# One feed-forward pass over both segments in the first layer, and the two halves of the recurrence's inverse extended separately

## What is computed

```python
h_lat = h_lat + m_lat[5] * channel_mixer(_modulate(_rms_norm(h_lat, norm_ffn[i]), m_lat[3], m_lat[4]))
if update_ctx:
    h_ctx = h_ctx + m_ctx[5] * channel_mixer(_modulate(_rms_norm(h_ctx, norm_ffn[i]), m_ctx[3], m_ctx[4]))

def _swiglu(h, w1, w3, w2):
    return (jax.nn.silu(h @ w1) * (h @ w3)) @ w2
```

## Time and profile before

| | us |
|---|---|
| median of three runs | 3259.41 |
| lowest and highest of them | 3255.51, 3261.84 |
| the profiled execution's own time | 3247.96 |
| its span, first to last instruction | 3246.2 |
| TensorE busy, share of the span | 3035.9, 94% |
| VectorE busy | 2022.0, 62% |
| ScalarE busy | 1500.8, 46% |
| mean granted TensorE clock | 0.967 |

### The profile page before, as it was taken

One profiled execution on the slowest core, in us unless ns is written; L12 is line 12 of the kernel. 1 busy time (PEld: TensorE's weight loads), 2 busy tenths in 40 slices (PEclk: granted clock), 3 DMA queues, 4 the chain that ended last, 5 costly groups with the idle time before them and its releaser, 6 DMA issues.

```text
span 3246.2 us, 70881 instructions
## 1 busy us (share of the span) xinstructions
PE 3035.9 (94%) x28960; PEld 2343.0 (72%) x28960; DVE 2022.0 (62%) x3676; ACT 1500.8 (46%) x2394; POOL 7.7 (0%) x17
## 2 busy tenths in 40 slices
PE   5988897989999989989999999999999999999998
PEld 3866684878989977643333333359988999998998
DVE  3768757565555552766666666666685666667566
ACT  3334223223444442646666666664447444445543
POOL 0000000000000000000000000000000000000000
PEclk8998898999999999989999999999999999999999
DMA  5232205004545552059999999955542555543454
GB/s 212 97 130 111 106 3 227 4 25 139 181 155 175 182 180 91 21 224 379 379 378 389 377 380 407 373 229 184 181 143 99 181 182 172 182 155 122 145 181 155
DMA packets 132792, 619.71 MB, mean 191 GB/s; under 512 B 14496, under 2 KB 18080, under 8 KB 98400
## 3 DMA queue, kind: packets, MB, share of 16 engines
q1 hardware_dynamic: 132048, 610.18, 51.5%
q0 software_dynamic: 528, 6.43, 0.5%
HBM read 615.50 MB, written 1.05 MB: 190 GB/s over the span
## 4 chain that ended last, share of the span: by engine, by line
PE 82%; DVE 10%; ACT 3%; DMA 2%; issue 1%; SPq 1%; DVEq 0%; ACTq 0%
PE ps L2443 21%; PE ps L310 16%; PE ps L311 16%; PE ps L312 16%; DMA ada_late<-wada 1%; PE ps L1777 1%; PE ps L864 1%; DVE w_lo L273 1%; PE ps L1774 1%; PE ps L1768 1%; PE ps L2454 1%; DVE tt L1865 1%; ACT w_hi L269 1%; DVE mxv L2157 1%; PE ps L792 0%
## 5 line engine op out<-in xcount | busy, mean ns | idle before, releaser
L273 DVE TENSOR_TENSOR w_lo<-w_raw,w_hi 128x1024 fp32r<-128x1024 f32 x529 | 646.3, 1224 | 598.3 <-ACT w_hi L269 594.7
L310 PE MATMUL ps<-a_hi,w_hi 128*128 128x256 f32 (+1 forms) x3012 | 899.1, 299 | 48.4 <-DVE a_lo L811 11.9
L311 PE MATMUL ps<-a_lo,w_hi 128*128 128x256 f32 (+1 forms) x3012 | 895.2, 297 | 0.0
L312 PE MATMUL ps<-a_hi,w_lo 128*128 128x256 f32 (+1 forms) x3012 | 894.4, 297 | 0.0
L269 ACT ACTIVATE w_hi<-w_raw 128x1024 fp32r<-128x1024 f32 x529 | 557.7, 1056 | 610.4 <-PE ps L312 556.3
L310 PEld LDWEIGHTS ps<-a_hi,w_hi 128*128 128x128 f32 x3012 | 578.2, 192 | 71.9 <-issue 45.4
L312 PEld LDWEIGHTS ps<-a_hi,w_lo 128*128 128x128 f32 x3012 | 573.0, 190 | 16.1
L311 PEld LDWEIGHTS ps<-a_lo,w_hi 128*128 128x128 f32 x3012 | 573.2, 190 | 15.2 <-issue 0.5
L2625 DVE COPY wx<-wset 128x512 f32 x1188 | 425.1, 422 | 223.1 <-PE ps L2443 208.0
L2565 ACT ACTIVATE wx<-wset 128x512 f32 x792 | 444.4, 621 | 214.7 <-PE ps L2443 206.3
L2443 PE MATMUL ps<-wx,xT 128*32 128x512 f32 x2640 | 377.6, 596 | 4.8 <-DVE wx L2625 4.8
(11 more groups left out here) (518 smaller groups left out, 3444.1 us busy)
## 6 DMA issues: line engine op xcount, KB each, us to landing
w_raw<-wstream SPq DMA_DIRECT2D x529, 512.0 KB, 3.3
wset<-wexp SPq DMA_DIRECT2D x264, 1024.0 KB, 7.8
ada_late<-wada SPq DMA_DIRECT2D x80, 512.0 KB, 6.2
ada_raw<-wada SPq DMA_DIRECT2D x16, 512.0 KB, 9.2
bia<-bias POOLq DMA_DIRECT2D x1, 4096.0 KB, 13.4
con<-consts SPq DMA_DIRECT2D x1, 1824.0 KB, 16.0
conb<-constsb POOLq DMA_DIRECT2D x1, 1224.0 KB, 5.7
hT<-ctxT SPq DMA_DIRECT2D x1, 1024.0 KB, 12.3
```

Source lines behind the costliest of these rows:

```text
L273: nc.vector.tensor_tensor(wlo[:, slot, :], raw[:, slot, :], whi[:, slot, :].bitcast(F32), ALU.subtract).then_inc(lo_ready.sem, 1)
L310: nc.tensor.matmul(out, lhs[0], rhs[0], start=start, stop=False, skip_group_check=skip)
L311: nc.tensor.matmul(out, lhs[0], rhs[1], start=False, stop=False, skip_group_check=skip)
L312: return nc.tensor.matmul(out, lhs[1], rhs[0], start=False, stop=stop, skip_group_check=skip)
```

## The change

Both segments go through the first layer's feed-forward in one pass. The stream has one entry `ffn` of 66 tiles in place of two. One norm of 512 columns precedes it (the routines that the attention's norm uses). All 44 tiles of `w1` and `w3` go first, alternately, each with 24 matmuls of 512 columns into bank 5, 6 or 7 in rotation; the 22 hidden blocks of both segments are all kept, in new tiles `gs_hi` and `gs_lo`. Then come 22 tiles of `w2` in a new order, with output group m as the outer index: one bank per group, filled completely over 22 hidden blocks before the next group begins. Group m's sum is added to `hT` as soon as it is complete. The engines' lists for this pass are written out without loops.

In the recurrence, half 1 of each level goes to bank 6+d in place of the second half of bank 2+d. VectorE adds the halves with two instructions of 256 columns. The add of half 0 raises `lv_in` itself. The add of half 1 raises a new signal `t1_in`, on which TensorE waits before it uses `tt` as an operand of L1774 and L1777 in the next level.

```diff
-STREAM = [("w_in", 27), ("w_out", 8), ("ffn_ctx", 3 * FT), ("ffn_lat", 3 * FT), ("qkv", 24),
+STREAM = [("w_in", 27), ("w_out", 8), ("ffn", 3 * FT), ("qkv", 24),
...
+        def pe_ffn_both(pe, base):
+            a = a_cols([CTX, LAT])
+            def chunk(t, k, out, operand, first, last):
+                slot = (base + t) % RING
+                w = (whi[:, slot, k * P:(k + 1) * P], wlo[:, slot, k * P:(k + 1) * P])
+                return pe_triple(out, w, operand, first, last)
+            def h_chunk(t, k):
+                last = chunk(t, k, ps[:, 5 + (base + t) % RING, :], a(k), k == 0, k == KT - 1)
+                if k == KT - 1:
+                    last.then_inc(tile_used.sem, 1)
...
+            for t in range(RING, 2 * FT):
+                pe.wait_ge(lo_ready.sem, base + t + 1)
+                f, third = divmod(t - RING, 2)
+                pe.wait_ge((S("g_f") if third else S("silu_ready")).sem, f + 1)
+                for k in range(KT):
+                    h_chunk(t, k)
+            for t in range(2 * FT, 3 * FT):
+                pe.wait_ge(lo_ready.sem, base + t + 1)
+                for j in range(KT):
+                    m, f = divmod((t - 2 * FT) * KT + j, FT)
+                    if m == 0 and j == 0:
+                        pe.wait_ge(S("g_ready").sem, min(f + KT, FT))
+                    last = chunk(t, j, ps[:, m, :], (gs_hi[:, f, :], gs_lo[:, f, :]), f == 0, f == FT - 1)
+                    if j == KT - 1:
+                        last.then_inc(tile_used.sem, 1)
+                    elif f == FT - 1:
+                        last.then_inc(*S("pair_out").one)
...
+        def dve_ffn_both(dve, link, base):
+            for t in range(3 * FT):
+                if t >= 1:
+                    dve_split(dve, base + t + LEAD, (base + t + LEAD) % RING)
+                if t < 2 * FT and t % 2 == 1:
+                    f = t // 2
+                    dve.wait_ge(S("silu_ready").sem, f + 1)
+                    dve.wait_ge(tile_used.sem, used(base, t))
+                    nc.vector.tensor_tensor(gf2[:, f % 2, :], sil2[:, f % 2, :], ps[:, 5 + (base + t) % RING, :],
+                                            ALU.mult).then_inc(S("g_f").sem, 1)
...
+                for m in range(KT):
+                    if 2 * FT + (m * FT + FT - 1) // KT == t:
...
+                        for s in (CTX, LAT):
+                            dst = hT[:, m, seg_cols(s)]
+                            ins = nc.vector.scalar_tensor_tensor(dst, ps[:, m, seg_cols(s)], m_col(0, 5, m, s), dst,
+                                                                 ALU.mult, ALU.add)
...
@@ pe_solve
                 for d in range(2):
                     pe.wait_ge(*S("x_sb").next("pe"))
+                    if lv > 0:
+                        pe.wait_ge(*S("t1_in").next("pe"))
                     if lv < RLEV - 1:
                         heads_of(d, lambda d, m, e: nc.tensor.matmul(
                             ps[hp(e), 2 + d, col(m)], tt[hp(e), d, 1, m, :], xs[hp(e), d, m, :],
-                            start=True, stop=True))
+                            start=True, stop=True)).then_inc(*S("t_ps").one)
                     heads_of(d, lambda d, m, e: nc.tensor.matmul(
-                        ps[hp(e), 2 + d, col(m, 1)], xs[hp(e), d, m, :], tt[hp(e), d, 1, m, :],
-                        start=True, stop=True)).then_inc(*S("t_ps").one)
+                        ps[hp(e), 6 + d, col(m)], xs[hp(e), d, m, :], tt[hp(e), d, 1, m, :],
+                        start=True, stop=True)).then_inc(*S("t1_ps").one)
@@ dve_solve
                 for d in range(2):
-                    dve.wait_ge(*S("t_ps").next("dve"))
                     if lv < RLEV - 1:
-                        t2_ = tt[:, d, :, :, :].rearrange("p s m l -> p (s m) l")
-                        link(nc.vector.tensor_tensor(t2_, t2_, bank(2 + d, 0, 8), ALU.add))
-                        dve.sem_inc(S("lv_in").sem, 1)
-                    else:
-                        nc.vector.tensor_tensor(tt[:, d, 1, :, :], tt[:, d, 1, :, :], bank(2 + d, 1), ALU.add
-                                                ).then_inc(*S("tT_done").one)
+                        dve.wait_ge(*S("t_ps").next("dve"))
+                        nc.vector.tensor_tensor(tt[:, d, 0, :, :], tt[:, d, 0, :, :], bank(2 + d), ALU.add
+                                                ).then_inc(*S("lv_in").one)
+                    dve.wait_ge(*S("t1_ps").next("dve"))
+                    nc.vector.tensor_tensor(tt[:, d, 1, :, :], tt[:, d, 1, :, :], bank(6 + d), ALU.add
+                                            ).then_inc(*S("t1_in" if lv < RLEV - 1 else "tT_done").one)
@@ the order of the stages, TensorE
-            for s, nm in ((CTX, "ffn_ctx"), (LAT, "ffn_lat")):
-                pe_norm(pe)
-                pe_ffn(pe, BASE[nm], s, FT)
+            pe_norm2(pe)
+            pe_ffn_both(pe, BASE["ffn"])
             pe_norm2(pe)
             pe_qkv(pe)
```

More of the change, by code:

```diff
@@ L110 @@
           "x_out": ("st_ps", 6), "slot_ps": ("g_ps", 8), "slot_sb": ("mb_rt", 1), "moe_free": ("mb_r", 1), "x_scaled": ("e1", 16),
+          "t1_ps": ("bc_ps", 16), "t1_in": ("wm", 16),
           "r_ready": ("e2", 16), "r_ps": ("dd", 16)}
@@ L365, in a_cols @@
             return lambda k: (a_hi[:, k, c], a_lo[:, k, c])
[L369 to L420, removed]
@@ L617, in dve_ffn_late @@
             split(3 * F - 1, 3 * F - 1)
+        def pe_ffn_both(pe, base):
[8 more added lines that the diff above has]
+                    last.then_inc(tile_used.sem, 1)
+            for j in range(RING):
+                pe.wait_ge(lo_ready.sem, base + j + 1)
+            for j, k in head_order(range(RING)):
+                if j == 0:
+                    pe.wait_ge(*S("alo_ready").next("pe"))
+                h_chunk(j, k)
+            for t in range(RING, 2 * FT):
[15 more added lines that the diff above has]
+                        last.then_inc(*S("pair_out").one)
+            gcount["pe"] += FT
@@ new lines, in act_ffn_both @@
+        def act_ffn_both(act, base):
+            for t in range(3 * FT):
+                if t >= 1:
+                    n = base + t + LEAD
+                    act_split(act, n, n // RING, n % RING)
+                if t < 2 * FT and t % 2 == 0:
+                    f = t // 2
+                    act.wait_ge(tile_used.sem, used(base, t))
+                    if f >= 2:
+                        act.wait_ge(S("g_f").sem, f - 1)
+                    nc.scalar.activation(sil2[:, f % 2, :], ps[:, 5 + (base + t) % RING, :], ACT.Silu
+                                         ).then_inc(S("silu_ready").sem, 1)
+            gcount["act"] += FT
@@ new lines, in dve_ffn_both @@
+        def dve_ffn_both(dve, link, base):
+            for t in range(3 * FT):
+                if t >= 1:
+                    dve_split(dve, base + t + LEAD, (base + t + LEAD) % RING)
+                if t < 2 * FT and t % 2 == 1:
+                    f = t // 2
+                    dve.wait_ge(S("silu_ready").sem, f + 1)
+                    dve.wait_ge(tile_used.sem, used(base, t))
+                    nc.vector.tensor_tensor(gf2[:, f % 2, :], sil2[:, f % 2, :], ps[:, 5 + (base + t) % RING, :],
+                                            ALU.mult).then_inc(S("g_f").sem, 1)
+                    dve.wait_ge(S("g_f").sem, f + 1)
+                    nc.vector.tensor_copy(gs_hi[:, f, :], gf2[:, f % 2, :]).then_inc(S("g_hi").sem, 1)
+                    dve.wait_ge(S("g_hi").sem, f + 1)
+                    nc.vector.tensor_tensor(gs_lo[:, f, :], gf2[:, f % 2, :], gs_hi[:, f, :].bitcast(F32),
+                                            ALU.subtract).then_inc(S("g_ready").sem, 1)
+                for m in range(KT):
+                    if 2 * FT + (m * FT + FT - 1) // KT == t:
+                        if (m * FT + FT - 1) % KT == KT - 1:
+                            dve.wait_ge(tile_used.sem, used(base, t))
+                        else:
+                            dve.wait_ge(*S("pair_out").next("dve"))
+                        for s in (CTX, LAT):
+                            dst = hT[:, m, seg_cols(s)]
+                            ins = nc.vector.scalar_tensor_tensor(dst, ps[:, m, seg_cols(s)], m_col(0, 5, m, s), dst,
+                                                                 ALU.mult, ALU.add)
+                            if s == CTX:
+                                link(ins)
+                        ins.then_inc(*S("h_ready").one)
+            gcount["dve"] += FT
@@ L619, in build @@
         gcount = {"pe": 0, "act": 0, "dve": 0}
         xcount = {"act": 0}
[L622 to L689, removed]
@@ L826, in build @@
         normw2 = sb("normw2", [P, KT, T2], at=arena)
+        gs_hi = sb("gs_hi", [P, FT, T2], F32R, at=arena + 4 * KT * T2)
+        gs_lo = sb("gs_lo", [P, FT, T2], F32R, at=arena + 4 * KT * T2 + 4 * FT * T2)
+        sil2 = sb("sil2", [P, 2, T2], at=g_at)
+        gf2 = sb("gf2", [P, 2, T2], at=g_at + 8 * T2)
```

(20 more changed lines are left out.)

## The result

The changed kernel takes 3222.9 us (median of four runs, 3222.0 to 3224.1) against 3260.6 of the kernel before in the same comparison (3255.5 to 3263.5). The ratio is 0.9886, 95% interval 0.9871 to 0.9902, so the gain is 37.7 us with an interval of 32 to 42. The forecast was 3229, and the measured time lies inside the range of 3218 to 3243. In a later comparison on one chip the same kernel stood at 3219.8 against 3257.1, ratio 0.9890 (0.9875 to 0.9905).

The account below looks back on a forecast made before the run. TensorE, busy 94% of the span, was taken as the bound. Feed-forward 19.2 us plus recurrence 11.2 us made 30.4 us, taken from the median 3259.4 to give 3229 us, range 3218 to 3243.

Parts of the forecast that it names:

- What bounds the kernel: Whole kernel: TensorE, busy 94% of the span, is the bound; halving weight splits and loads is worth nothing by itself.
- The pace: Feed-forward: 3168 narrow matmuls at 0.1200 us become 1584 wide ones at 0.2333 us, a gain of 10.6 us.
- The edges: Feed-forward: one norm of 13.97 us replaces 7.77 and 12.61; with its norm the pass takes 386.1 instead of 405.3 us.
- The recurrence: Levels of the recurrence: period falls from 3.40 to 3.05 us, over 32 transitions, a gain of 11.2 us.
- The reason inside the level: Recurrence level: half 0's add of 256 columns, 0.42 us, right after its group lets TensorE's products start at 0 and 0.467.
- the spare of 0.08 us for direction 1: Recurrence level: VectorE signals direction 1's first add at about 3.44 us, needed at 3.52.
- The sum and the median: Whole kernel: 19.2 + 11.2 = 30.4 us saved, taken from the median 3259.4 rather than the profiled 3247.96, giving 3229 us.
- VectorE late: Rival, recurrence levels: VectorE's in-order list misses the spare; full loss of that gain gives 3240 us; chance 0.14.
- Wide no faster: Rival, feed-forward pass: wide matmuls no faster than narrow, with operands from two large new tiles; 3240 us; chance 0.06.
- The rule's pace: Rival, feed-forward pass: 512 columns run at the skill page's 0.216 us; 3201 us; chance 0.02.
- Starvation: Rival, feed-forward pass: TensorE's list without loops waits for instructions; at 0.7 us a tile, 3275 us; chance 0.04.
- No effect: Rival, the passes: some dependence, such as tiles sharing memory, serialises them to no gain; 3255 to 3260 us; chance 0.02.

Follow-up runs that it names:

- narrow matmuls: Changed kernel, but each wide feed-forward product done as two of 256 columns with the same weight; 3232.3 us, ratio 0.9937 to the kernel before.
- short norms: Changed kernel with its two norms beside the feed-forward summed in four strips, root and reciprocal on 128 columns; 3211.4 us, ratio 0.9862 to the kernel before.
- late add: Changed kernel, but VectorE adds half 0 only when both halves of its direction are there; 3227.1 us, ratio 0.9921 to the kernel before.
- written-out loops: Kernel before with the loops of its two feed-forward passes written out on TensorE, ScalarE and VectorE, nothing else; 3257.1 us, ratio 1.0009.

## Why the prediction was right, and where it was off

**What bounds the kernel.** Right. Halving the weight splits and the loads shows in busy time and DMA share and in no wait of TensorE, and it leaves the pass at 382.2 us while the matmuls stay narrow.

**The pace.** Right: 0.2333 us per wide start in the changed pass, and 10.1 us come back when only the width is undone, against 10.6 from the two rows of before. The formula of the Trainium skill's page "TensorE: Matmul & The Clock Gate", section "Back-to-back issue gap" (an estimate of 0.2158 us at 512 columns), was not met here either. That section gives it for matmuls by themselves, while the stream here has a weight load for each. For such a stream it states about 131 ns at 512 columns, which the prediction left out and which is further still from the 233.3 ns measured.

**The edges.** The norm came at 13.97 and the pass at 372.1, both as stated. What the forecast did not see is that the narrow pair of passes is not always 405.3: two of four traces that have it show 407.8 and 407.9, because the clock sometimes falls to half in the inner gap earlier (0.53 against 0.73 over the sums). The gain is therefore 19 to 22 us and not 19.2. That is a term of the sum taken from one execution only.

**The recurrence.** The level period was put at 3.05 and is 3.03, but the count of what it applies to was wrong. An undisturbed call of the recurrence begins 33.39 or 33.47 us after the one before it in the old traces and 31.71 or 31.78 in the new ones, 1.69 less, where the sum had 4 x 0.35 = 1.4. Three transitions between levels gain 0.37 each (3.40 to 3.03). The first gains only 0.20 (2.53 to 2.33 from direction 1's first product), since direction 0's product of the first level was made 3 us ahead in both kernels. The fifth level gains 0.38: its first products no longer wait for VectorE, and its second group follows 1.65 instead of 2.03 us behind the level's start. The sum left that out. So 1.4 came close because one term was too large and another was missing.

Eight calls give 13.5 us. The stretch from first copy to norm is 400.7 to 403.9 us in the four traces with the old levels and 387.4 to 391.7 in five with the new ones (the last two from the runs of narrow matmuls, 391.4, and short norms, 387.9), 12 us apart in the mean and 9 to 16 from pair to pair. One reason is the granted clock: in every old trace two calls are long, the third and the seventh (22.4 to 22.7 us from first copy to `rh` against 21.1), and in the new ones two to four of the first seven. In the changed kernel's first trace they are the second, third and sixth, with 20.98, 20.75 and 20.75 us against 19.4. Its second trace has two, and its stretch is 13.5 us shorter than in the first trace of before (387.4 against 400.9). The window over the level that took 3.89 us there:

```profile
393.50:398.00 4.50, 4.21 (x90) 4.22 (x92) 2.43 (x7) 0.38 (x1) 0.00 (x0) 0.62 0.02 4
```

Why the clock falls in more calls of some traces was not tested.

**The reason inside the level** was half right. I put the gain down to the early add of half 0, and held the spare of 0.08 us for direction 1 to be the risk. The late add's trace shows that 0.28 us of lateness there costs 0.04 in a level and 0.27 in the last one, so VectorE being late was not close to deciding in that trace; its slower timed runs leave room for a larger cost. What limits a level is TensorE's six groups and one copy: with the copy hidden the period is the six groups, 2.80 us.

**The sum and the median.** 30.4 was stated, 35.8 to 37.7 was measured. About 2 us are the recurrence's miscounted levels (8 x 0.29), up to 2.5 the narrow passes' spread. The remaining 1 to 3 us are within the intervals, and no run assigns them.

**The rivals.** VectorE late: refuted, period 3.03. Wide no faster: refuted by the pace, 0.2333 us. The rule's pace: refuted by the same number. Starvation: refuted, 371.88 of 372 us busy, and the written-out loops cost nothing. No effect: refuted, the interval of the gain is 32 to 42 us.

## What to carry to other kernels

When two passes share weights and TensorE is the bound, price the merger by the distance between matmul starts at each width and by the gaps it removes, since saved loads and splits counted for nothing here. In a dependent chain of small steps, list what each step's first instruction waits for: once TensorE waits only for one short copy, issuing an independent product into that gap took the rest here (3.03 to 2.80 us a level). In a gap of the bound engine, look for work standing in front of the chain that nobody needs yet, like the weight split here.

## What the runs showed of the hardware

Two traces of one kernel differ by 4 us in a stretch behind every edit (2084.6 and 2088.7) and by 9 us in span (3246.2 and 3255.4), and across kernels a stretch that no edit touches took 355.2 to 362.6 us. The same 16 sums of a norm took 5.14 or 6.74 us, with a granted clock of 0.73 or 0.53 over them. In this case a single trace was sound for durations and periods, and too coarse for differences of whole spans below 10 us.
